# A kernel of two transformer blocks: expert-up's weight parts move eight words further in their ring

## What is computed

```python
def block_fn(args):
    hb, ib, gb = args
    u = expert_down[ib]
    act = jax.nn.gelu(jnp.einsum("td,thkd->thk", hb, u), approximate=False)
...
    # weighted with the gates, then back to width 1024 through expert_up[ib]
```

## Time and profile before

| | us |
|---|---|
| median of 3 runs | 1394.59 (1391.94 to 1396.21) |
| the profiled execution | 1393.0 |
| its span, first to last instruction | 1391.2 |
| mean granted clock | 0.997 of full speed |

### The profile page before, as it was taken

How to read it: one execution, slowest core, us unless ns; L and a number is a source line. 1 busy time by engine, 2 the same in 40 slices (tenths; PEclk the granted TensorE clock), 3 DMA queues, 4 the chain that set the end, 5 groups by cost and what they waited for, 6 DMA issues and landing times.

```text
span 1391.2 us, 32164 instructions
## 1 busy us (share of the span) xinstructions
PE 1361.8 (98%) x9828; PEld 1266.4 (91%) x9828; DVE 1040.3 (75%) x2235; ACT 886.2 (64%) x1855; POOL 651.0 (47%) x499
## 2 busy tenths in 40 slices
PE   7999999999999999999999999999999999999997
PEld 4799999999999978999999999999998888888886
DVE  7778868888887586429999868888876666666665
ACT  5668765555445655547888687777765555555554
POOL 4896792000005867688898987777730000000000
PEclk9999999999999999999999999999999999999999
DMA  9776575989983633554555554444456665566652
GB/s 349 275 243 228 198 259 186 327 317 318 336 317 118 218 122 113 190 216 168 183 183 184 183 169 153 160 156 151 155 165 194 195 195 190 191 193 195 193 191 85
DMA packets 79285, 283.84 MB, mean 204 GB/s; under 512 B 8821, under 2 KB 8949, under 8 KB 79098
## 3 DMA queue, kind: packets, MB, share of 16 engines
q1 hardware_dynamic: 79226, 283.07, 59.5%
HBM read 281.99 MB, written 1.05 MB: 203 GB/s over the span
## 4 chain that ended last, share of the span: by engine, by line
PE 79%; POOL 6%; issue 5%; DVE 4%; PEld 3%; ACT 2%; DMA 1%; PEldq 0%; SPq 0%; POOLq 0%; DVEq 0%; ACTq 0%
PE psA L1771 19%; PE psA L1774 19%; PE psA L1775 19%; PE psD L1771 6%; POOL w_lo L563 6%; PE psD L1774 5%; PE psD L1775 5%; PE psD L2230 1%; PEld psA L1771 1%; PE psD L2231 1%; PEld psA L1775 1%; PEld psA L1774 1%; PE psA L1792 1%; DVE arena L1503 1%; DMA xT<-x 1%
## 5 line engine op out<-in xcount | busy, mean ns | idle before, releaser
L620 ACT CAST w_hi<-raw 128x512 fp32r<-128x512 f32 x864 | 529.2, 620 | 426.5 <-PE psA L1771 308.3
L563 POOL TENSOR_TENSOR w_lo<-raw,w_hi 128x512 fp32r<-128x512 f32 x476 | 633.7, 1351 | 352.8 <-ACT w_hi L620 343.0
L1771 PE MATMUL psA<-h_hi,w_hi 128*128 128x256 f32 x1568 | 452.9, 289 | 0.6 <-POOL w_lo L563 0.5
L1774 PE MATMUL psA<-h_lo,w_hi 128*128 128x256 f32 x1568 | 443.0, 283 | 0.0
L1775 PE MATMUL psA<-h_hi,w_lo 128*128 128x256 f32 x1568 | 442.9, 282 | 0.0
L1070 DVE TENSOR_TENSOR w_lo<-raw,w_hi 128x512 fp32r<-128x512 f32 x388 | 266.1, 691 | 153.6 <-ACT w_hi L620 151.9
L1771 PEld LDWEIGHTS psA<-h_hi,w_hi 128*128 128x128 f32 x1568 | 300.0, 191 | 4.1 <-issue 1.5
L1774 PEld LDWEIGHTS psA<-h_lo,w_hi 128*128 128x128 f32 x1568 | 300.2, 191 | 0.1
L1775 PEld LDWEIGHTS psA<-h_hi,w_lo 128*128 128x128 f32 x1568 | 299.9, 191 | 0.0
L1771 PE MATMUL psA<-w_hi,u_hi 128*128 128x512 f32 x512 | 199.3, 389 | 0.4 <-DVE u_lo L1128 0.4
L1774 PE MATMUL psA<-w_lo,u_hi 128*128 128x512 f32 x512 | 199.2, 389 | 0.0
(11 more groups left out here) (381 smaller groups left out, 2136.2 us busy)
## 6 DMA issues: line engine op xcount, KB each, us to landing
raw<-expert_down SPq DMA_DIRECT2D x128, 512.0 KB, 3.2
raw<-expert_up SPq DMA_DIRECT2D x128, 512.0 KB, 4.3
arena<-ada SPq DMA_DIRECT2D x96, 512.0 KB, 5.2
raw<-gateup SPq DMA_DIRECT2D x44, 512.0 KB, 5.3
raw<-feat SPq DMA_DIRECT2D x28, 512.0 KB, 3.6
raw<-win SPq DMA_DIRECT2D x24, 512.0 KB, 3.3
raw<-down SPq DMA_DIRECT2D x22, 512.0 KB, 6.4
raw<-wout SPq DMA_DIRECT2D x20, 512.0 KB, 3.2
```

Of the source, the lines that this page charges most:

```text
L563: nc.gpsimd.tensor_tensor(w_lo[:, s * HALF:(s + 1) * HALF], raw_half(n), w_hi[:, s * HALF:(s + 1) * HALF].bitcast(F32), ALU.subtract).then ...
L620: nc.scalar.copy(w_hi[:, n % SLOTS * HALF:(n % SLOTS + 1) * HALF], raw_half(n)).then_inc(hi_ready, 1)
L1771: first = mm(o, w[0], m[0], start=start, stop=False, skip_group_check=True)
L1774: mm(o, w[0], m[1], start=False, stop=False, skip_group_check=True)
```

## The change

From its third unit on, expert-up's weight parts are written and read through `up_hi` and `up_lo`, which are the rings `w_hi` and `w_lo` moved by `LINE // 2` = 8 words (32 bytes). The first two units still use `w_hi` and `w_lo`. Behind each ring 16 words of padding are put in, so that the last place has room; `w_lo` so moves by 16 words, and all that lies behind it in the map by 32, multiples of 16 both.

A moved place overlaps the first eight words of the next old one. So the copies of the third unit's two halves and of the fourth unit's first half wait for one more half to be begun by PE (`crosses`). On ACT the first four of these units are written out ahead of the loop, whose number of turns falls from 31 to 30.

To make room, `eps` and `pos_i` move into unused words of `late`, which is cut from 2304 to 2272 words, and four other small tensors move within it. `late` so begins at a multiple of 16 words, and so do `rinv` and `rms`.

```diff
+        LINE = 16
+        MAP = 4096 + 2048 + 2048 + 2048 + 2048 + 4096 + 2 * LINE + 32768
...
+        RAW, HI, LO, X_AT, M_AT, H_AT, ARENA = (
+            0, 4096, 6144 + LINE, 8192 + 2 * LINE, 10240 + 2 * LINE, 12288 + 2 * LINE, 16384 + 2 * LINE)
...
+        up_hi = at_place("up_hi", HI + LINE // 2, SLOTS * HALF, F32R)
+        up_lo = at_place("up_lo", LO + LINE // 2, SLOTS * HALF, F32R)
...
-        eps = sb("eps", [P, 1])
-        late = sb("late", [P, 2304])
+        late = sb("late", [P, 2272])
...
-            def split_half():
+            def split_half(dst=w_hi, crosses=0):
...
-                    act.wait_ge(half_used, halves.value(SLOTS) + next_stage.n)
+                    act.wait_ge(half_used, halves.value(SLOTS) + next_stage.n + crosses)
...
-            def next_expert(j, slot):
-                split(1)
+            def next_expert(j, slot, crosses=0):
+                split_half(up_hi, 1 if crosses >= 1 else 0)
+                split_half(up_hi, 1 if crosses >= 2 else 0)
                 u_upper(j, slot)
...
-            with repeat(act, (P - 4) // 4, {halves: 8}) as i:
+            for j in range(4):
+                next_expert(2 + j, (2 + j) % 4, max(2 - j, 0))
+            with repeat(act, (P - 8) // 4, {halves: 8}) as i:
                 for j in range(4):
-                    next_expert(i * 4 + (2 + j), (2 + j) % 4)
+                    next_expert(i * 4 + (6 + j), (2 + j) % 4)
...
-                    lower_weights()
+                    lower_weights(1, up_hi, up_lo)
...
-                expert(j, j + 1, first=j == 0)
+                expert(j, j + 1, first=j == 0, places=(w_hi, w_lo) if j < 2 else (up_hi, up_lo))
```

More of the change, by code:

```diff
@@ L197, in two_mixers_program @@
         psD = ctx.enter_context(nc.psum_tensor("psD", [P, BANKS, 512], F32))
-        MAP = 4096 + 2048 + 2048 + 2048 + 2048 + 4096 + 32768
+        LINE = 16
+        MAP = 4096 + 2048 + 2048 + 2048 + 2048 + 4096 + 2 * LINE + 32768
         sb("map", [P, MAP])
@@ L205, in at_place @@
             return nc.alloc_sbuf_tensor_at(name, [P, n], dt, offset=map_at + 4 * at)
-        RAW, HI, LO, X_AT, M_AT, H_AT, ARENA = 0, 4096, 6144, 8192, 10240, 12288, 16384
+        RAW, HI, LO, X_AT, M_AT, H_AT, ARENA = (
+            0, 4096, 6144 + LINE, 8192 + 2 * LINE, 10240 + 2 * LINE, 12288 + 2 * LINE, 16384 + 2 * LINE)
         raw = at_place("raw", RAW, SLOTS * 1024)
@@ L222, in two_mixers_program @@
         scale_cols = sb("scale_cols", [P, 2, KC])
-        eps = sb("eps", [P, 1])
-        late = sb("late", [P, 2304])
-        late_at = nc.sbuf_base - 4 * 2304
+        late = sb("late", [P, 2272])
+        late_at = nc.sbuf_base - 4 * 2272
         taken = [0]
@@ L352, in two_mixers_program @@
         r_i, r_f, r_abs, r_e, r_u, r_t, r_l, r_s = [row(i) for i in range(8)]
-        small = part(late, 2048, 256)
+        small = part(late, 2048, 224)
         m_cols = part(small, 0, 2, MH, NT)
@@ L362, in two_mixers_program @@
         both_w = part(small, 208, KC, 2)
[L363 to L366, removed]
+        roots = part(small, 120, 2, NT)
+        inverses = part(small, 124, 2, NT)
+        eps_both = part(small, 194, 1)
+        one_root = part(small, 195, 1)
         posf = part(small, 200, 2)
@@ L371, in two_mixers_program @@
         x_diag = rinv[:, :].rearrange("p (t n) -> p t n", t=NT)
-        pos_i = sb("pos_i", [P, NT], I32)
+        pos_i = part(small, 196, NT).bitcast(I32)
+        eps = part(small, 198, 1)
         scores = part(arena, 28672, NT, 2 * QH, NK)
@@ L432, in _ @@
             sp.dma_start(c_one, c[:, :]).then_inc(sem("c_in"), 16)
-            sp.dma_start(pos_i[:, :], pos[:, :]).then_inc(sem("pos_in"), 16)
+            sp.dma_start(pos_i, pos[:, :]).then_inc(sem("pos_in"), 16)
             sp.dma_start(bias_rows[0:TOK_BLOCKS, 0:512], bias_tok[:, :]).then_inc(sem("bias_in"), 16)
@@ L619, in split_half @@
                     act.wait_ge(raw_full[n // 2 % SLOTS], at if halves.loop is None else halves.loop * 2 + at)
-                nc.scalar.copy(w_hi[:, n % SLOTS * HALF:(n % SLOTS + 1) * HALF], raw_half(n)).then_inc(hi_ready, 1)
+                nc.scalar.copy(dst[:, n % SLOTS * HALF:(n % SLOTS + 1) * HALF], raw_half(n)).then_inc(hi_ready, 1)
             def split(n_units=1):
@@ L1060, in _, with lower_weights @@
             lows = Count()
-            def lower_weights(n_units=1):
+            def lower_weights(n_units=1, high=w_hi, low=w_lo):
                 for _ in range(2 * n_units):
@@ L1069, in lower_weights @@
                     w = slice(n % SLOTS * HALF, (n % SLOTS + 1) * HALF)
-                    V.tensor_tensor(w_lo[:, w], raw[:, n % 8 * HALF:(n % 8 + 1) * HALF], w_hi[:, w].bitcast(F32),
+                    V.tensor_tensor(low[:, w], raw[:, n % 8 * HALF:(n % 8 + 1) * HALF], high[:, w].bitcast(F32),
                                     ALU.subtract).then_inc(lo_ready, 1)
@@ L1131, in _ @@
             dve.wait_ge(sem("pos_in"), 16)
-            own(V.tensor_copy(posf, pos_i[:, :]))
+            own(V.tensor_copy(posf, pos_i))
             for t in range(NT):
@@ L1749, in _, with half @@
             norms = Count()
-            def half():
+            def half(high=w_hi, low=w_lo):
                 n = halves.n
@@ L1756, in half @@
                 s = slice(n % SLOTS * HALF, (n % SLOTS + 1) * HALF)
-                return w_hi[:, s], w_lo[:, s]
+                return high[:, s], low[:, s]
             def begun(ins):
@@ L2243, in _, with expert @@
             stage_ends()
-            def expert(j, n, first=False, last=False):
+            def expert(j, n, first=False, last=False, places=(up_hi, up_lo)):
                 pe.wait_ge(sem("u_lo"), n)
@@ L2250, in expert @@
                 for h in range(2):
-                    w = half()
+                    w = half(*places)
                     for t in range(NT):
```

## The result

The changed kernel takes 1399.83 us (median of 12 runs) against 1393.99 for the kernel before (12 runs): 5.8 us more, where 4.1 less were forecast. The means stand at 1.0049 to 1, with an interval of 1.0038 to 1.006. So it is slower by half a per cent, clear of the noise.

A forecast was written before the change was run, and what follows sets the result against it. PE's matmul pace was taken to bound the kernel; -5.0 us for the move and +0.9 for the waits, the rest 0, gave -4.1 us, 1390.5 us from a median of 1394.6, with a range of 1384 to 1402.

The forecast's parts named there:

- What bounds the kernel: Whole span: PE, busy for 98%, sets the time; in expert-up its pace is 226.6 ns and its feeders wait for it.
- The move, -5.0 us: Expert-up from the third unit: 1512 matmuls with moving operand 8 words off each gain 3.3 ns, as in proj.
- The bound from above, 230 ns: Upper bound of the move: the unsettled 512-column pace in the first token stage, +3.4 ns or +5.1 us.
- The note against the term: Against the move: weight loads take 192 ns at pace 120.0, 188 at 116.7, and in expert-up 188 already.
- The padding, 0: Operands moved by 16 or 32 words: no cost taken; bounds 19 us either way over 5856 matmuls of 256 columns.
- The waits, +0.9 us: Crossing to moved places: PE stops 0.8 us at the third unit, next step 0.1 more; fourth unit just in time.
- The copies at moved places, 0: Copies and subtractions to and from moved places: idle time of 0.59 us on ACT, 0.50 on DVE hides longer ones.
- (C): Expert-up never settles and keeps the early token stage's 230 ns: +6.0 us, 1400.6; chance 0.16.
- (B): Expert-up's pace stays at 226.6 ns, only the wait is left: +0.9, 1395.5 us; chance 0.19.
- (D): Expert-up's extra over its columns goes altogether: -16.6 us, 1378; chance 0.11.
- (E): Expert-up gets part of the gain, 1 to 2 ns, as PE changes between two states: 1392 to 1394.5; chance 0.06.
- The page's rule: Weight loads have their own read port and take no SBUF bandwidth from a running matmul; so 8 words change nothing.

The follow-up runs named there:

- matmuls alone: Small program, not the kernel: groups of three matmuls, operands laid chosen words off, no other engine working; 226.7 ns at 0 words, 233.4 at 8 with 512 columns.
- h 48 words off: Against the kernel before: 48 words of padding ahead of h and the arena only, small tensors as in the changed kernel; 1371.82 us, 0.9838 of before.

## Why the prediction was wrong

- **What bounds the kernel** was right: PE's pace and nothing that feeds it. The feeders' waits are there after as before.
- **The move, -5.0 us**, is the step that failed, with its ground: "the extra is per matmul and not per column, and proj's 280 take 8 cycles off it". Two column counts with the same extra at 0 words had been taken for one rule, and 8 words were then carried from 256 columns to 512. Alone they cost 512 columns 6.7 ns, +10.1 us, and in the changed kernel, padding included, 8.9 ns or +13.5 us. The bound from above, 230 ns, was too low for either. The note against the term, that the loads are at 188 ns already, pointed the right way, but a load's record doesn't tell a good place from a bad one here: it is 188 to 189 ns in the changed expert-up as well.
- **The padding, 0**, failed too. "If the line that counts were longer than 16 words" was named as a bound and set aside because three stages at multiples of 256 words agree (the rows show two, expert-down and wout2). They could not tell: all of them have the distance 0 modulo 64. The padding alone costs expert-up 4.5 ns, with the 8 words it is 8.9 (the two don't add up, and matmuls alone have the same 235.5 at these places), and it moved the other stages too: 14.4 us went in expert-up, the median is only 5.8 up, so if expert-up costs the same in the median execution, some 8.6 came back elsewhere.
- **The waits, +0.9 us**, were right in place, releaser and size, in the changed kernel and alone: 0.8 for the stop, 0.1 for the step after it, and the fourth unit just in time. Alone they cost 1.1 in all, inside the bounds of 0.7 to 1.2.
- **The copies at moved places, 0**, were right: ACT still idles 149.5 / 234 = 0.64 us ahead of each.
- **The rivals.** (C) gave the sign and, with 1400.6, nearly the time, but by luck and not by its mechanism. PE does settle, on a pattern that repeats every three matmuls, at 235.5 and not at 230; what came back elsewhere (14.4 - 5.8 = 8.6 us) made the time fit. (B), (D) and (E) fell: expert-up is at neither 226.6 nor anything below it, and no place that was tried with 512 columns is below 226.7.
- **The page's rule.** "TensorE: Matmul & The Clock Gate" of the Trainium skill, section "Step-by-step: what each phase is for", says that loading the next weights takes no SBUF read bandwidth from a running matmul. The runs of matmuls alone speak against it: with all else equal the distance between the two operands changes the pace from 226.7 to as much as 236.9 ns, and the 8 words that should have changed nothing by the prediction's reading of the pages cost 10.1 us by themselves. That the reads of the two collide would be one reason for that, but it is only argued; no run shows it.

What stays open: why 64 words, why the sign counts, and what picks one of several settled paces.

## What to carry to other kernels

Before a row of one shape is carried to another, look for a row of that shape at the place in question; where there is none, the sign is open too, and a small program of that one instruction at many places shows the paces that can occur; which of them a kernel then keeps it may not tell. Padding is a change of its own: whatever lies behind it moves against whatever lies ahead. And when the bounding engine gets faster in a stage, look for the slow chain beside it that was just in time; it takes the gain back in one stop and in the lower clock behind it.

## What the runs showed of the hardware

- The pace of float32 products whose two operands alternate between weight loads and matmuls depends on the distance of the two in words modulo 64, sign included: from 226.7 to 236.9 ns for 512 columns (the latter at 1 word) and from 113.3 to 120.0 for 256. The clock was 1.00 in both runs of matmuls alone.
- 512 columns are best at 0 words (226.7) and 256 columns worst there (120.0), with 24 words no better; 384 columns have 173.3 at 0, 8 and 16 and 176.0 at 32.
- One set of places can have several settled paces, 117.7 and 113.2 (h 48 words off, ahead of the picking and behind it) or 116.7 and 120.0; one can be kept over 100 us, and in the changed kernel a group of other matmuls in between changes from one to the other. The twelve executions of the changed kernel lie between 1397.1 and 1406.3 us, those of before between 1391.7 and 1396.2; that the settled paces are the reason is not shown.
- After a stop of 6.2 us the granted clock was 0.83 over 780 to 800 us, between its two levels, and PE did 99 matmuls there where it did 169 without the stop.
